# Encoder block on eight cores: the first sequence is read in halves of 256 positions, summed for its norm on TensorE, and projected in a new order

## The chip, the cores and the metric

The kernel runs on the eight cores of one Trainium2 chip. Each core works alone on two of sixteen sequences; no core talks to another. The metric is the device time in microseconds (us) of the slowest core, as a median of several runs. A profile is one execution, shown for the slowest core. The engines of a core are named as in the profile: PE (TensorE matmuls), PEld (its weight loads), ACT (ScalarE), DVE (VectorE), POOL (GpSimd) and SP (SyncE, which here only issues transfers). Each engine has its own queue and works through it in order; SPq, ACTq and POOLq are the queues as issuers of transfers.

## What is computed

One layer of a bidirectional encoder for x of 16 x 2048 positions x 1024 channels, in fp32 at the interface and bf16 in the matmuls:

```
h = RMSNorm(x)
[u | q | k | v | g_f | g_a] = h @ w_in        # 256 | 768 | 768 | 768 | 1024 | 1024
y_f = (real part of the 2-D DFT of u over positions and group channels) @ fourier_mix
y_a = three dilated windowed attentions (dilation 1, 4, 16; 4 heads of 64 each),
      partial rotary on q and k, combined by their softmax denominators
x = x + (sigmoid(g_f) * (y_f @ w_f) + sigmoid(g_a) * (y_a @ w_a)) @ w_mix_out
x = x + CrossAttn(RMSNorm(x), RMSNorm(mem))    # mem: 256 x 1024 per sequence
x = x + SqReLU_MLP(RMSNorm(x))                 # 1024 -> 4096 -> 1024
out = RMSNorm(x)
```

## The kernel before

All tensors lie with channels on the 128 partitions: `hT[:, c, t]` is channel chunk c of 8, position t of 2048. Every on-chip tile is a view of one buffer, the `arena`; a small planner (`Prog`) keeps the order of the program on each engine and adds a wait wherever two operations touch the same 256 bytes (or the same PSUM bank). Since a helper records every operation, all instructions carry line 148 (line 146 for groups of small transfers).

The two sequences run one after the other (`for b_ in range(nseq)`). For each: projection of u and of q, k of attention group 0 (256 columns each); v of group 0 (`v_unit`, 8 units); the DFT as folds on DVE (`folds`), a channel step (`z_unit`, `zx_unit`) and a position step (`dft_unit`, `dft_mid`); the rotary step, for which `gather` copies rows of q and k to a strip `rot` by 8 transfers on SP, `rotate` works on the strip on DVE, and 8 more transfers (kept in `back`) bring it home; attention group 0 with the projections of group 1 woven in (`interleave(attn(0), proj_gen(1), ...)`), then groups 1 and 2; the gates and branches (`gate_mm`, `branch`, n from 0 to 31, with the end of the attention, `combine`, still running on ACT and DVE when they begin); output projection, cross-attention, MLP. The second sequence's first norm is computed during the first sequence's MLP (`load_st`, `sq_st`, `load_xh`, `fin_next`), so its projection starts from a ready `hT`. The first sequence has nothing to hide behind, and the first stage of the program is its norm and projection.

In that first stage, x comes in four tiles `xin[tg]` of 512 positions, the first two in two halves of 256 columns. `norm1_sq` squares each of the 8 channel chunks on ACT and adds them in fp32 on DVE and POOL in two partial sums, splits the sum into a high and a low bf16 part, and `norm_rstd` adds over partitions with two matmuls against `ones`, followed by Ln and Exp on ACT; `norm_apply` writes `hT` with 8 DVE instructions. The projection is six units a tile (`u_unit` twice, `qk_unit` four times), each 8 matmuls into one PSUM bank and one copy on ACT. A list of hooks says after which unit the next norm's parts are put in. The memory's norm (`mem_sq`, `mem_fin`) is hooked to the last tile. Weights come by transfers of POOL's queue that also turn fp32 into bf16 (`aload(i)`: slice i of `wa`; 0 is u, 1 to 3 are q, k, v of group 0, 4 to 6 of group 1, 7 to 9 of group 2; `bload(i)` the larger ones). `aload(1)` and `aload(2)` stand behind POOL's additions of the first two halves, and the third and fourth tile of x wait for `aload(2)` to land.

The softmax here doesn't subtract the row's maximum and nothing guards it: scores larger than these inputs give would overflow.

## Time and profile before

| | |
|---|---|
| median of 3 runs (lowest to highest) | 2097.21 us (2095.4 to 2100.14) |
| the profiled execution's own time | 2097.6 us |
| its span, slowest core (core 7) | 2096.6 us |
| spans of the eight cores | 2087.0 to 2096.6 us |
| PE busy share of the span | 95% |
| mean granted clock of TensorE, by core | 0.981 to 0.985 |

The span runs from the first to the last instruction of the core; the time has 1.0 us more around it. A waiting row says which engine waited for which, in total, how many times, and the longest. A timeline row gives start, duration, engine, operation with its tile shapes and count, and in brackets how long the engine had been idle before it and who ended that. A row of windows gives busy time and count of each engine in a stretch, then the granted clock (1.00 is 2.4 GHz, 0.50 is 1.2 GHz), the busy share of the 16 transfer engines, and what they moved in GB/s.

### The profile page before, as it was taken

To read this page: it belongs to the slowest core of one execution; us is meant where nothing else is said; L and a number is where in the kernel's file an instruction comes from. 1 tells how busy PE (TensorE), PEld (TensorE's weight loads), DVE (VectorE), ACT (ScalarE), POOL (GpSimd) and SP (SyncE) were. 2 spreads that over 40 slices of the span, in tenths; PEclk is the share of its full clock that TensorE was granted. 3 is DMA by queue.
4 is the path that set the end of the run, shared out by engine and by line. 5 is a ranking of instruction groups with operands and counts; after the bars stand their busy time and mean duration, and the time that the engine had idled before them with its cause. 6 is when DMAs were issued, how large, how long until landed. Compare 5 with 4: busy or idle time off the path is not lost.

```text
span 2096.6 us, 30871 instructions; the slowest of 8 cores (2087.0 to 2096.6 us)
## 1 busy us (share of the span) xinstructions
PE 1983.2 (95%) x10282; PEld 973.3 (46%) x10282; DVE 982.1 (47%) x1586; ACT 770.7 (37%) x1309; POOL 418.5 (20%) x391
## 2 busy tenths in 40 slices
PE   4879979999999999999999997999999999999996
PEld 2445534455444444444445563445544444444443
DVE  4554663355554333334875467225645433333354
ACT  4434552246542143212434555224654211111243
POOL 2200013253240033100340001325314000000033
PEclk9999989999999999999999999999999999999998
DMA  8532226066100244223456322606610022222112
GB/s 208 126 76 61 48 40 194 1 112 117 34 21 40 41 121 109 52 61 72 142 140 151 61 41 41 201 1 107 121 36 1 1 41 41 41 41 41 21 71 91
DMA packets 40524, 155.43 MB, mean 74 GB/s; under 512 B 4785, under 2 KB 19250, under 8 KB 30130
## 3 DMA queue, kind: packets, MB, share of 16 engines
q0 software_dynamic: 11808, 75.50, 20.5%
q1 hardware_dynamic: 28128, 77.61, 11.9%
q8 instruction: 87, 1.43, 0.3%
q14 instruction: 67, 0.55, 0.1%
q10 hardware_dynamic: 434, 0.35, 0.1%
HBM read 205.87 MB, written 16.78 MB: 106 GB/s over the span
## 4 chain that ended last, share of the span: by engine, by line
PE 85%; DVE 5%; ACT 3%; issue 3%; DMA 2%; POOL 1%; SPq 1%; ACTq 0%; DVEq 0%; POOLq 0%
PE ps L148 85%; DVE arena L148 5%; ACT arena L148 3%; DMA arena<-arena 1%; POOL arena L148 1%; DMA arena<-x 1%; SPq L146 0%; DMA arena<-wa 0%; ACT L148 0%; ACTq L142 0%; DVEq L142 0%; SPq L148 0%; POOLq L142 0%; SPq L142 0%
## 5 line engine op out<-in xcount | busy, mean ns | idle before, releaser
L148 PE MATMUL ps<-arena 128*128 128x512 bf16 (+4 forms) x10282 | 1983.2, 355 | 105.3 <-ACT arena L148 57.6
L148 PEld LDWEIGHTS ps<-arena 128*128 128x128 bf16 (+1 forms) x10282 | 973.3, 100 | 1114.9 <-issue 188.7
L148 ACT ACTIVATE arena<-ps 128x512 bf16<-128x512 f32 (+4 forms) x812 | 488.9, 625 | 970.9 <-PE ps L148 803.9
L148 DVE TENSOR_TENSOR arena<-arena 128x512 bf16<-128x512 bf16 (+8 forms) x607 | 310.5, 531 | 604.2 <-ACT arena L148 586.2
L148 POOL TENSOR_TENSOR arena<-arena 128x512 f32<-128x512 f32 (+2 forms) x299 | 364.2, 1219 | 769.0 <-ACT arena L148 517.1
L148 DVE TENSOR_TENSOR arena<-ps,arena 128x512 f32<-128x512 f32 (+3 forms) x376 | 294.4, 791 | 244.2 <-PE ps L148 243.2
L148 ACT ACTIVATE arena<-arena 128x512 f32<-128x512 f32 (+3 forms) x451 | 261.3, 589 | 320.3 <-DVE arena L148 214.8
L148 DVE SCALAR_TENSOR_TENSOR arena<-arena 128x512 bf16<-128x512 f32 (+3 forms) x328 | 218.0, 707 | 51.0 <-ACT arena L148 50.5
L148 POOL DMA_DIRECT2D arena<-wb x62 | 33.6, 544 | 674.2 <-PE ps L148 674.1
L148 DVE SCALAR_TENSOR_TENSOR arena<-arena,ps 128x512 f32<-128x512 f32 x128 | 82.1, 684 | 151.7 <-PE ps L148 149.1
L148 DVE SCALAR_TENSOR_TENSOR arena<-ps,arena 128x512 f32<-128x512 f32 x64 | 43.5, 688 | 32.5 <-PE ps L148 32.5
L148 POOL DMA_DIRECT2D arena<-wa x20 | 10.9, 554 | 115.3 <-PE ps L148 113.9
L148 POOL MEMSET arena<- 128x2048 bf16 x6 | 10.9, 1812 | 109.3 <-PE ps L148 109.3
L148 ACT ACTIVATE arena<-ps,arena 128x512 f32<-128x512 f32 (+1 forms) x37 | 23.6, 637 | 24.8 <-PE ps L148 22.0
L148 DVE CAST arena<-ps 128x512 bf16<-128x512 f32 (+1 forms) x36 | 20.5, 582 | 11.8 <-PE ps L148 11.3
L148 DVE COPY arena<-ps 128x1024 f32<-128x1024 f32 (+3 forms) x20 | 20.2, 1010 | 6.6 <-PE ps L148 6.6
L148 DVE STREAM_SHUFFLE arena<-arena 128x2048 bf16<-128x2048 bf16 x6 | 13.7, 2288 | 0.0
L148 ACT ACT_TABLE_LOAD x9 | 11.5, 1283 | 2.9 <-PE ps L148 1.6
L148 DVE LOAD_MASK_SELECT arena<-arena x6 | 0.1, 14 | 7.2 <-DMA arena<-arena 7.2
L148 DVE CAST arena<-arena 128x1 bf16<-128x1 f32 (+1 forms) x9 | 1.4, 160 | 0.4
L148 DVE MEMSET arena<- 128x1 bf16 (+2 forms) x6 | 0.8, 130 | 1.2 <-PEq L211 1.1
L211 POOL MEMSET const-float32-0.0<- 128x1 f32 x1 | 0.1, 98 | 0.5 <-issue 0.5
(3 smaller groups left out, 0.3 us busy)
## 6 DMA issues: line engine op xcount, KB each, us to landing
arena<-wb POOLq DMA_DIRECT2D x62, 1024.0 KB, 10.1
arena<-x SPq DMA_DIRECT2D x40, 512.0 KB, 3.9
arena<-x SPq DMA_DIRECT2D x8, 2048.0 KB, 13.8
out<-arena SPq DMA_DIRECT2D x28, 512.0 KB, 2.7
arena<-wa POOLq DMA_DIRECT2D x20, 512.0 KB, 9.8
arena<-rope SPq DMA_DIRECT2D x6, 1024.0 KB, 9.7
arena<-arena SPq DMA_DIRECT2D x96, 64.0 KB, 2.3
arena<-x SPq DMA_DIRECT2D x16, 256.0 KB, 10.3
```

Of the source, the lines that this page charges most:

```text
L148: ins = getattr(eo, o['name'])(*o['args'], **o['kw'])
L211: nc = bass.Bass("TRN2", target_bir_lowering=False)
```

## The change

The input x is laid out as eight contiguous pieces of 256 positions a sequence instead of four of 512, and every transfer that reads x follows this. The rest concerns the first stage, the stage behind it, and one place in the gate stage:

- x of the first sequence is loaded as 8 halves (of 1 MB; SP issues half i once half i-2 has landed), the weights of u, q and k at once at the start, the other weights of the stage behind the last half, most constants behind half 5; `ones` is written by DVE.
- The squares go to bf16 tiles `sqb` by two ACT instructions of 1024 columns a half, and the sum over channels is taken by 8 matmuls against `ones` into one bank (`half_rstd`); the additions on DVE and POOL and the split in two parts are gone. `half_sum` does nothing.
- The projection works by halves: `tiles('uq', i)` keeps four banks open and walks over the channel chunks, `tiles('k', i)` two. Norms run one half ahead.
- `warm(n)` issues n matmuls of 128x512 whose result is not used: 10 at the start, 4 ahead of the first projection, 34 ahead of `branch(0)` in each sequence.
- Behind the projection the channel step is woven into the last four units of v, the DFT's position step follows directly, mostly in banks 2 to 5, and the memory's norm is finished there; the transfers of `aload(7)`, `bload(0)`, `bload(1)` and the next rotary table wait for `back`.

```diff
-    cb[:, 0:128] = 1.0
...
-    for name, shp, dt in [('x', [nseq, NTG, 128, 4096], F32), ('mem', [nseq, 128, 2048], F32),
+    for name, shp, dt in [('x', [nseq, 8, 128, 2048], F32), ('mem', [nseq, 128, 2048], F32),
...
         def load_consts():
             OP('dve', 'memset', eps, 1e-6, writes=[eps])
+            OP('dve', 'memset', ones, 1.0, writes=[ones])
+            OP('dve', 'memset', ones32, 1.0, writes=[ones32])
             act(rstd[:, 0:1], eps, AF.Square)
-            for q, dst, src in ((0, cb, dr['cb']), (1, gains, dr['gains'].rearrange("p (n c) -> p n c", n=5)),
-                                (2, fm32, dr['fmix']), (3, altrow[0:1, :], dr['altrow'])):
-                dma('act', dst, src, 'c%d' % q)
+            dma('act', gains, dr['gains'].rearrange("p (n c) -> p n c", n=5), 'c1')
             OP('dve', 'memset', Wz, 0.0, writes=[Wz])
+            warm(10)
+
+        def warm(n):
+            o = psf(P.bank())
+            for _ in range(n):
+                mm(o, ones, view(c0 + 2048, 512), True, True)
+
+        def load_consts2():
+            for q, dst, src in ((0, cb[:, 128:642], dr['cb'][:, 128:642]), (2, fm32, dr['fmix']), (3, altrow[0:1, :], dr['altrow'])):
+                dma('sp', dst, src, 'c%d' % q)
...
-        def norm_apply(gi, srcs, dsts, n=512):
+        def norm_apply(gi, srcs, dsts, n=512, r=None):
             for c in range(8):
-                stt(dsts[c], srcs[c], gains[:, gi, c:c + 1], rstd[:, 0:n], ALU.mult, ALU.mult)
+                stt(dsts[c], srcs[c], gains[:, gi, c:c + 1], rstd[:, 0:n] if r is None else r, ALU.mult, ALU.mult)
...
+        XOFF = [M0 + 16 * KB, M0 + 24 * KB, Y0, Y0 + 8 * KB] + [X0 + i * KB for i in (16, 24, 32, 40)]
+        xin = [view(o, 2048, F32, pat="p (c t) -> p c t", c=8) for o in XOFF]
+
+        def xpair(off, c):
+            return view(off, 4096, F32, pat="p (h c t) -> p h c t", h=2, c=8)[:, :, c, :]
+
+        def x_half(b_, i):
+            return dr['x'][b_, i].rearrange("p (c t) -> p c t", c=8)
+
+        xin_op = {}
+
+        def load_xin(i, parts=2):
+            for h in range(parts):
+                cs = slice(h * 8 // parts, (h + 1) * 8 // parts)
+                xin_op[i] = dma('sp', xin[i][:, cs, :], x_half(0, i)[:, cs, :], 'xin%d%d' % (i, h),
+                                [xin_op[i - 2]] if i > 1 else ())
+
+        sqb = [view(o, 2048) for o in (X0 + 48 * KB, X0 + 56 * KB, T0)]
+        ones32 = view(OFF['memn'], 128, F32)
+
+        def half_sq(i, parts=2, src=None):
+            n = 2048 // parts
+            src = (xin[i] if src is None else src).rearrange("p c t -> p (c t)")
+            for p in range(parts):
+                act(sqb[i % 3][:, p * n:(p + 1) * n], src[:, p * n:(p + 1) * n], AF.Square)
+
+        def half_sum(i):
+            q = sqb[i % 3]
+            return
+
+        def half_r(i):
+            return rstd[:, i % 2 * 256:i % 2 * 256 + 256]
+
+        def half_rstd(i, chunks=8):
+            o = psf(P.bank())[:, 0:256]
+            for c in range(chunks):
+                mm(o, ones, sqb[i % 3][:, c * 256:(c + 1) * 256], c == 0, c == chunks - 1)
+            act(half_r(i), o, AF.Ln, scale=1.0 / D, bias=eps)
+            act(half_r(i), half_r(i), AF.Exp, scale=-0.5)
+
+        def half_apply(i):
+            norm_apply(0, [xin[i][:, c, :] for c in range(8)], [hT[:, c, i * 256:(i + 1) * 256] for c in range(8)],
+                       256, half_r(i))
...
-                load_xin(0, 0, 0, 256)
+                load_xin(0, parts=4)
                 aload(0)
                 load_consts()
-                load_xin(0, 0, 256, 256)
-                load_xin(0, 1, 0, 256)
-                load_xin(0, 1, 256, 256)
-                norm1_sq(0, 0, ns=0, t0=0, n=256, eng=0)
-                norm1_fin(0, 0, 0, 0, 256)
                 aload(1)
-                norm1_sq(0, 0, ns=1, t0=256, n=256, eng=0)
-                wk = aload(2)
-                load_xin(0, 2, after=[wk])
-                load_xin(0, 3)
+                aload(2)
+                for i in range(1, 8):
+                    load_xin(i)
+                    if i == 5:
+                        load_consts2()
                 load_rope(0)
...
-            memst = view(X0 + 32 * KB, 2048, F32, pat="p (c m) -> p c m", c=8)
+            memst = view(Y0 + 8 * KB, 2048, F32, pat="p (c m) -> p c m", c=8)
...
-                tb = [ssacc, rstd][odd]
+                tb = view(T0 + 4096 + odd * 2048, 512, F32)
...
+                def tiles(which, i):
+                    tn = slice(i * 256, i * 256 + 256)
+                    us = [(aslot('uqk'.index(w)), j, psf(P.bank())[:, 0:256], w) for w in which for j in range(2)]
+                    for dc in range(8):
+                        for w, j, o, _ in us:
+                            mm(o, w[:, dc, j * 128:(j + 1) * 128], hT[:, dc, tn], dc == 0, dc == 7)
+                    for _, j, o, w in us:
+                        if w == 'u':
+                            act(uT[:, j, tn], o, AF.Copy)
+                        else:
+                            cp('act', qkv_views(0)['qk'.index(w)][:, j, tn], o)
+
+                half_sq(0, parts=4)
+                half_rstd(0, 8)
+                half_apply(0)
+                half_sq(1)
+                warm(4)
+                tiles('uq', 0)
+                half_sq(2)
+                half_rstd(1, 8)
+                half_apply(1)
+                half_sq(3)
+                half_sum(3)
+                aload(3, [xin_op[7]])
+                tiles('uq', 1)
+                half_rstd(2, 8)
+                half_apply(2)
+                tiles('k', 0)
+                tiles('k', 1)
+                for i in range(2, 8):
+                    if i < 7:
+                        half_rstd(i + 1)
+                        half_apply(i + 1)
+                    if i == 2:
+                        half_sq(4)
+                        half_sum(4)
+                    tiles('uq', i)
+                    if i < 5:
+                        half_sq(i + 3)
+                        half_sum(i + 3)
+                    if 3 < i < 7:
+                        aload(i, [xin_op[7]])
+                    if i == 6:
+                        v_ones(0)
+                        load_dft()
+                    if i == 7:
+                        make_wz()
+                        half_sq(8, src=memst)
+                        half_sum(8)
+                    tiles('k', i)
...
             for i in range(8):
                 v_unit(0, 2 * i, ALLB)
+                if i == 5 and b_ == 0:
+                    half_rstd(8)
+                if i > 3:
+                    z_unit(i - 4, 0)
             zx_unit()
-            for i in range(4):
-                z_unit(i, 0)
-                z_unit(i, 1)
+            LB = (2, 3, 4, 5)
+            z_unit(0, 1)
+            z_unit(1, 1)
+            dft_unit(0, 0, ALLB)
+            z_unit(2, 1)
+            z_unit(3, 1)
+            dft_unit(0, 1, LB)
+            dft_mid(LB)
+            dft_unit(1, 0, LB)
+            dft_unit(1, 1, LB)
+            if b_ == 0:
+                norm_apply(2, [memst[:, c, :] for c in range(8)], [memn[:, c, :] for c in range(8)], 256, half_r(8))
             v_ones(1)
-            bload(0)
-            bload(1)
-            load_rope(1)
+            if b_ == 0:
+                aload(7, back.values())
+            bload(0, back.values())
+            bload(1, back.values())
+            load_rope(1, back.values())
...
-            for j in range(2):
-                for odd in range(2):
-                    dft_unit(j, odd, ALLB)
-            dft_mid(ALLB)
...
+                if n == 0:
+                    warm(34)
                 branch(n)
                 if n == 6:
                     for tg in range(NTG):
-                        dma('sp', xT[:, tg], dr['x'][b_, tg].rearrange("p (c t) -> p c t", c=8), 'xr%d' % tg)
+                        for h in range(2):
+                            dma('sp', xT[:, tg, :, h * 256:(h + 1) * 256], x_half(b_, 2 * tg + h), 'xr%d%d' % (tg, h))
...
-                for h in range(4):
-                    dma('sp', xst[:, 2 * h:2 * h + 2, :], dr['x'][b_ + 1, tg].rearrange("p (c t) -> p c t", c=8)[:, 2 * h:2 * h + 2, :], 'st%d' % h)
+                for h in range(2):
+                    dma('sp', xst[h], x_half(b_ + 1, 2 * tg + h), 'st%d' % h)
...
-                norm_sq(fc, xst[:, fc, :], ns=1)
+                norm_sq(fc, xpair(M0 + 16384, fc), ns=1)
...
+                dma('sp', xh[i % 3], x_half(b_ + 1, i), 'xh%d' % (i % 3))
...
-    xl = x.reshape(B, NTG, 512, 8, 128).transpose(0, 1, 4, 3, 2).reshape(B, NTG, 128, 4096)
+    xl = x.reshape(B, 8, 256, 8, 128).transpose(0, 1, 4, 3, 2).reshape(B, 8, 128, 2048)
```

## Rows read from the trace of the kernel before

**Rows 1.** Windows: first projection, v of group 0, then up to the first attention.

```profile
0.00:98.20 98.20, 60.96 (x308) 32.67 (x309) 47.62 (x90) 44.47 (x111) 27.88 (x38) 0.91 0.72 175
98.20:112.20 14.00, 13.99 (x129) 12.29 (x126) 11.00 (x23) 6.28 (x12) 0.00 (x0) 1.00 0.23 40
112.20:135.24 23.04, 11.26 (x78) 5.69 (x79) 14.30 (x21) 7.67 (x15) 2.86 (x3) 0.91 0.68 126
```

**Rows 2.** Waits of PE up to 98 us: in total, times, longest.

```profile
PE ps L148 <- ACT arena L148: 26.1, 6, 17.7
PE ps L148 <- DVE arena L148: 9.7, 13, 2.2
```

**Rows 3.** The chain that ended last: first transfer of x.

```profile
2.56 12.11 DMA arena<-x
```

**Rows 4.** Timeline of the first stage: one instruction or run of each kind.

```profile
20.66 1.06 PE L148 MATMUL ps<-arena 128*128 128x256 bf16 x3 [2.11 <-DVE arena L148]
...
29.65 3.25 DVE L148 SCALAR_TENSOR_TENSOR arena<-arena 128x256 bf16<-128x256 f32 x8 [1.77 <-ACT arena L148]
...
32.37 4.53 PE L148 MATMUL ps<-arena 128*128 128x256 bf16 x40 [0.56 <-DMA arena<-wa]
...
37.07 1.19 ACT L148 ACTIVATE arena<-ps 128x256 bf16<-128x256 f32 x4
...
43.29 0.47 ACT L148 ACTIVATE arena<-ps,arena 128x256 f32<-128x256 f32 x1
...
69.76 4.31 ACT L148 ACTIVATE arena<-arena 128x512 f32<-128x512 f32 x8
```

**Rows 5.** Transfer queues up to 100 us: packets, MB, share of 16 engines.

```profile
q1 hardware_dynamic: 5936, 12.58, 43.7%
q0 software_dynamic: 1152, 4.19, 25.8%
```

**Rows 6.** Windows inside the first stage.

```profile
46.00:52.00 6.00, 5.88 (x25) 3.34 (x25) 4.75 (x12) 4.12 (x9) 0.74 (x1) 0.50 1.04 238
52.00:54.00 2.00, 2.00 (x19) 1.70 (x17) 2.00 (x2) 0.16 (x1) 1.80 (x2) 0.91 1.10 199
...
66.00:68.00 2.00, 1.71 (x4) 0.31 (x3) 2.00 (x4) 0.00 (x0) 0.00 (x0) 0.51 0.63 125
```

**Rows 7.** Timeline from the end of the projection to the first attention.

```profile
96.69 15.50 PE L148 MATMUL ps<-arena 128*128 128x512 bf16 x135
...
100.67 3.26 DVE L148 SCALAR_TENSOR_TENSOR arena<-arena 128x256 bf16<-128x256 f32 x8 [2.88 <-ACT arena L148]
...
115.30 2.06 PE L148 MATMUL ps<-arena 128*128 128x128 bf16 x27 [0.39 <-DVE arena L148]
...
117.86 3.69 DVE L148 TENSOR_TENSOR arena<-arena 128x2048 bf16<-128x2048 bf16 x3 [0.17 <-DVE arena L148]
...
118.86 7.74 PE L148 MATMUL ps<-arena 128*128 128x512 bf16 x41 [0.60 <-ACT arena L148]
...
135.24 15.09 PE L148 MATMUL ps<-arena 64*128 64x192 bf16 x69 [8.65 <-DMA arena<-arena]
```

**Rows 8.** Small transfers of the rotary step, median to landing: 118 to 140 us.

```profile
arena<-arena SPq DMA_DIRECT2D x8, 64.0 KB, 10.2
```

**Rows 9.** The same transfers over the whole span (the page).

```profile
arena<-arena SPq DMA_DIRECT2D x96, 64.0 KB, 2.3
```

**Rows 10.** Timeline of PE at the first branches, first sequence, then second.

```profile
304.14 8.06 PE L148 MATMUL ps<-arena 128*128 128x512 bf16 x27 [8.11 <-ACT arena L148]
...
1285.15 12.78 PE L148 MATMUL ps<-arena 128*128 128x512 bf16 x52 [2.27 <-DVE arena L148]
1301.88 10.35 PE L148 MATMUL ps<-arena 128*128 128x512 bf16 x40 [3.96 <-ACT arena L148]
```

**Rows 11.** Timeline of ACT behind v in the second sequence.

```profile
1129.41 4.67 ACT L148 ACTIVATE arena<-ps 128x512 bf16<-128x512 f32 x10 [1.15 <-PE ps L148]
```

**Rows 12.** Window of the gate stage behind the second reading of x.

```profile
340.00:345.00 5.00, 5.00 (x25) 2.25 (x23) 1.31 (x3) 1.68 (x3) 1.26 (x1) 1.00 0.00 0
```

More of the change, by code:

```diff
@@ L340, in norm_sq, with like @@
             acc_, hi, lo = acc_[:, 0:n], hi[:, 0:n], lo[:, 0:n]
+            def like(a):
+                return a if len(src.shape) == 2 else a.rearrange("p (h t) -> p h t", h=2)
             if isinstance(eng, int):
@@ L346, in norm_sq @@
                 b = sq4[k % 4][:, 0:n]
-                act(part if k < 2 else b, src, AF.Square)
+                act(like(part if k < 2 else b), src, AF.Square)
                 if k > 1:
@@ L358, in add @@
                     tt(eng, acc_, acc_, sq[i % 2][:, 0:n], ALU.add)
-            act(sq[k % 2][:, 0:n] if k else acc_, src, AF.Square)
+            act(like(sq[k % 2][:, 0:n] if k else acc_), src, AF.Square)
             if lag and k:
@@ L411, in build_program @@
         rope = view(R0 + 32768, 4096, pat="p (k t) -> p k t", k=2)
-        xin = [view(o, 4096, F32, pat="p (c t) -> p c t", c=8) for o in (M0 + 16384, Y0, X0 + 16 * KB, X0 + 32 * KB)]
-        def load_xin(b_, tg, t0=0, n=512, after=()):
-            src = dr['x'][b_, tg].rearrange("p (c t) -> p c t", c=8)
-            i = tg
-            return [dma('sp', xin[i][:, 2 * h:2 * h + 2, t0:t0 + n], src[:, 2 * h:2 * h + 2, t0:t0 + n],
-                        'xin%d%d%d' % (i, h, t0), after) for h in range(4)]
@@ L431, in build_program, with load_rope @@
         rsw = view(X0 + 60 * KB, 2048)
[L433 to L434 removed]
+        def load_rope(g, after=()):
+            dma('sp', rope, dr['rope'][g].rearrange("p (k t) -> p k t", k=2), 'rope', after)
         pend = []
@@ L1079, in load_xh @@
             def load_xh(i):
-                tg, t0 = i // 2, i % 2 * 256
-                for h in range(2):
-                    dma('sp', xh[i % 3][:, 4 * h:4 * h + 4, :],
-                        dr['x'][b_ + 1, tg].rearrange("p (c t) -> p c t", c=8)[:, 4 * h:4 * h + 4, t0:t0 + 256], 'xh%d%d' % (i % 3, h))
+                dma('sp', xh[i % 3], x_half(b_ + 1, i), 'xh%d' % (i % 3))
             def fin_next(tg, b_=b_):
```

40 lines of the change are left out of this document (2 added, 38 removed).

## The prediction

> **What bounds the kernel now.** I began with the windows by stage [rows 1], because a busy share over the whole span hides where PE stands idle. The reader is to see that the first 98.2 us hold 61.0 us of PE work, and that the 23 us ahead of the first attention hold 11.3 us; the 14 us of v between them are full. A window of the gate stage [rows 12] shows PE busy all the time, as most of the rest; there only matmuls count, and no part of the change removes one of those. What can be gained lies in the two stretches in front.
>
> The waits of PE in the first stretch [rows 2] say on whom: 26.1 us for ACT (17.7 of them at the start, when ACT itself waits for x) and 9.7 us for DVE. The chain [rows 3] begins with a transfer of x from 2.56 to 14.67 us; the first projection matmul runs at 20.66 [rows 4]. So 6.0 us pass from the landing of the first 256 positions to work for PE, and the same path of squares, additions, splitting, Ln, Exp and scaling stands ahead of every later half. Transfers are busy 72% of the stretch [rows 1]; the last x lands at about 67 us, where their share falls to 0.63 [rows 6]. By the queues [rows 5] plain transfers take 43.7 us of all engines for 12.58 MB, 3.47 us a MB, and the converting ones 25.8 us for 4.19 MB, 6.16 us a MB.
>
> In the second stretch PE waits 8.65 us at the end for the rotary strip's way home [rows 7], which took 10.2 us to land [rows 8] where the same transfers take 2.3 us over the span [rows 9]: two large weight loads and a table were issued beside them.
>
> **The change, part by part. The start.** One half of x (1.05 MB) costs 3.64 us of the queue, one converting load (0.52 MB) 3.23 us. Three converting loads now run beside the first halves instead of one. Half 0 can't land before 2.56 + 3.64 = 6.2 us, and before the change 14.7 us were needed; I take 11.5. From there: a square of 512 columns 0.54 (4.31 / 8), the last two sum matmuls 0.4, Ln 0.47, Exp no dearer, one scaling 0.41 (3.25 / 8) [rows 4], and five handoffs of 0.1: the projection starts at 14.4 and its 32 matmuls take 32 x 0.113 = 3.6 us (4.53 / 40), to 18.0. The additions on POOL and DVE and the split are gone from the path; the 8 sum matmuls cost PE 8 x 0.108 = 0.87 us a half (13.99 / 129 [rows 1]) where it had two.
>
> **The second half waits for the third.** In ACT's order the squares of half 2 stand ahead of Ln and Exp of half 1; while x of half 2 is missing, the norm of half 1 waits behind it. Until half 2 has landed the engines move 3.15 MB of x (10.9 us) and 1.57 MB of weights (9.7 us): 2.56 + 20.6 = 23.2 us; without the weights it would be 13.5. I take 23.2. Two squares of 1024 columns (at most 2 x 0.54 each) 2.1, Ln and Exp 0.9, one scaling 0.4: `tiles('uq', 1)` starts at 26.7.
>
> **From there PE is the bound.** A half costs PE 48 x 0.113 + 0.87 = 6.3 us; ACT 2.1 + six copies of 0.30 (1.19 / 4) + 0.9 = 4.8; DVE 3.3; the x queue 3.64. SP issues a half only when the one two before has landed, which keeps two in flight; x is through after 8.39 x 3.47 + 9.7 = 38.8 us, at about 42, ahead of need. Behind 26.7 come: `uq` of half 1 3.6, sum of half 2 0.9, `k` of halves 0 and 1 3.6, sum of half 3 0.9, six halves of 5.42 32.5, four sums 3.5, and the wait for `make_wz` ahead of the last `k`, which I put at 1.3 (its matmuls stand behind a DVE cast, as before): 46.3, to 73.0. Seven us of idle PE ahead of 26.7 may cost clock: between 46 and 52 us the granted clock was 0.50 and 25 matmuls of 256 took 6 us, when 19 took 2 right behind [rows 6]. At 0.113 they would have taken 2.8, so one such fall costs 3.2; I book half, 1.5. The projection ends at 74.5 instead of 98.2: **23.7 gained**; at best 66.7 (half 2 early, no fall, no wait for `make_wz`).
>
> **v to attention.** Before, 37.0 us (98.2 to 135.24). PE's work: v 14.0, channel step 32 x 0.076 = 2.4 (2.06 / 27 [rows 7]), memory sum 0.9, `zx` 0.3, position step 33 matmuls of 512 at 0.217 = 7.2, `dft_mid` 0.6: 25.4, and 2 for handoffs between short steps: 27.4. The other path is DVE's: folds and rotary step took 103.9 to 121.55, 17.6 us [rows 7], and start as the projection ends, since the memory's 8 scalings (3.26 us) no longer stand ahead. From the end of `rotate` to attention went 13.7 us, 10.2 of it landing and 3.5 issue; with 2.3 for landing it is 5.8. Sum 23.4, under PE's 27.4: the way home is hidden with 4 us to spare, and if it lands in 10.2 again it shows by 4. **9.6 gained**, between 7 and 11.6. What waits for `back` now: on POOL three weight loads with nothing due behind them until the next group's weights, on SP the rotary table, needed only near the end of attention group 0. So I cost these waits at nothing; the cover is that stage's PE work.
>
> **Small terms.** The memory's 8 scalings now lie on DVE ahead of the first attention masks: between 0 and 3.3, I take 1 lost. `warm(34)` is 34 x 0.217 = 7.4 us of PE. In the first sequence PE stood 8.11 us idle there, in the second 3.96 [rows 10]: nothing in the first, 3.4 in the second, less the slow matmuls after the idle time; I take 3 lost, between 0 and 7. In the second sequence half of the channel step's copies (4.67 us on ACT [rows 11]) goes beneath v, while PE's part of it, 1.2, lengthens v: 1 gained, between 0 and 3. The second reading of x now lands in rows of 1 KB; it is issued at n = 6 with 25 rounds of 20 matmuls (4.3 us each) ahead of its first use, and was through by 340 us with PE full [rows 12]: nothing, and even at half speed nothing. The contiguous loads in the MLP lie under full PE: nothing.
>
> **Sum.** 23.7 + 9.6 - 1 - 3 + 1 = 30.3 us off the profiled execution's 2097.6: 2067.3. The median shown is 0.4 below that execution: 2067.
>
> **Clock, row and rule.** The row shows 1.2 GHz for 6 us of which PE was busy 5.88, behind a stretch of short bursts, and then a rise to 0.91 of 2.4 GHz [rows 6]. The Trainium skill (TensorE: Matmul & The Clock Gate, section "HAM oscillation — how this bites in real kernels") says that a loop which waits between short bursts falls back at each wait, and that every burst then starts slow. By that rule the woven order could start half after half slow; the sum goes by the row, one fall booked by half, and the rule's case is the fifth way below.
>
> **The other ways it could go.** (1) As summed, 2060 to 2075. (2) Half 2 lands early and no clock falls: 66.7 and 25.4 behind it, 43.1 gained in the two stretches; with the small losses hidden and 2 from the second sequence 2052. For it speaks that squares and x overlap far better; against it the three converting loads at once. (3) x lands no earlier than before, at 67: then squares, sum, Ln, Exp and the last half's projection follow, 67 + 2.1 + 0.9 + 0.9 + 0.4 + 5.4 + 1.3 = 78.0, 3.5 worse, 2071; with two falls of the clock 2077. Against it: the first stretch moved x in rows of 1 or 2 KB, paused for `aload(2)`, and shared with five more weight loads that now wait. (4) The second stretch keeps its 37 us, because something else ends there last (the DFT matrix late, small transfers slow again): 2077. (5) Slower: PE stays at 1.2 GHz through the first stretch. Matmuls then double from 26.7 on, 45.0 more: 118.0, attention at 145.4, 10 later than before, with the small terms 2111. It decides when more than 70% of that work (31.8 of 45.0 us, where attention plus 3 reaches 135.24) runs slow; the rows show 0.91 as the stretch's mean clock with far more idle time, so it is unlikely. That nothing changes would need two of these in balance.
>
> **How the numbers follow.** Chances: (1) 0.55, (2) 0.15, (3) 0.14, (4) 0.11, (5) 0.03, no change 0.02. The time is that of (1), 2067. The worst of (3) with 30 us for the second stretch and `warm(34)` uncovered is 2087; the range from 2052 to 2080 leaves out the far ends of (2) and (3), and (5). Within 0.2% (4.2 us) counts as no change, about what a measurement of this kernel can tell: faster 0.95, same 0.02, slower 0.03.
>
> **What would show it.** In the profile after, the last projection matmul near 74 and the first of attention near 102; x landed by 45; PE without waits for ACT between 27 and 73; the strip's small transfers landing in 2 to 3 us; in the second sequence branches beginning some 3 us later against the end of attention. I am wrong if x lands after 60, if the granted clock is 0.50 for more than 10 us of the stretch, or if attention begins more than 32 us after the last projection.

## The result, and the profile after

| | before | after |
|---|---|---|
| time, median of the runs | 2097.66 us | 2058.13 us |
| ratio of the times, 95% interval | | 0.9809 [0.9773, 0.9844] |
| profiled execution | 2097.6 us | 2056.9 us |
| span of the slowest core | 2096.6 us (core 7) | 2055.9 us (core 1) |
| mean span of the 8 cores | 2091.7 us | 2053.3 us |

The forecast was 2067 us, from 2052 to 2080. The change is faster by 40 us, 9 more than forecast. The same kernel on another chip, beside the last experiments, gave a ratio of 0.9800 [0.9786, 0.9814]. The pages of before and after show different cores, and cores differ by some microseconds at the start, so the stages below are means over cores: a stage begins where a named instruction begins. On the chips of the experiments one die ran at a lower clock in many runs, so an experiment's means are over four cores of the other die (0 to 3, for the last four 4 to 7), in its profiled execution or, where it is said, in all executions in which that die kept its clock.

| start in us (mean) | first scaling | second half's scaling | first copy of v | to first Exp of attention | group 0: on to POOL's memset for group 2 | from there to the end | span |
|---|---|---|---|---|---|---|---|
| before | 19.9 | 29.7 | 100.6 | 34.3 | 60.0 | 1896.9 | 2091.7 |
| after | 20.4 | 29.6 | 79.1 | 23.5 | 56.8 | 1893.9 | 2053.3 |
| gained | -0.4 | 0.0 | 21.4 | 10.7 | 3.2 | 3.0 | 38.4 |
| forecast | 6 | 3 | 23.7 | 9.6 | 0 | -3 | 30.3 |

The columns after the third are durations and add up with it to the span. In the last row, the memory's scalings (-1) and `warm(34)` and the second sequence (-3 and +1) stand together.

The windows of core 1 answer to [rows 1]: the projection up to v, v, and up to the first Exp.

```profile
0.00:78.20 78.20, 60.20 (x470) 47.65 (x471) 28.92 (x78) 39.87 (x84) 5.88 (x12) 0.87 0.81 205
78.20:92.20 14.00, 14.00 (x137) 12.62 (x135) 12.97 (x25) 6.85 (x15) 0.00 (x0) 1.00 0.29 79
92.20:103.63 11.43, 11.43 (x83) 5.97 (x81) 8.14 (x10) 6.24 (x13) 1.80 (x1) 1.00 0.28 47
```

PE's busy time in the projection is as before (60.2 against 61.0 us); 19 us of idle time are gone. Behind v PE is now full, where it stood half idle. The idle time that is left lies ahead of 31 us. The timeline of PE on this core shows it, and below it PE's timeline behind 66 us and its waits up to 66 us, which answer to [rows 2].

```profile
2.19 4.08 PE L148 MATMUL ps<-arena 128*128 128x512 bf16 x10 [2.19 <-DVE arena L148]
...
19.35 2.29 PE L148 MATMUL ps<-arena 128*128 128x256 bf16 x6 [4.88 <-ACT arena L148]
22.06 4.90 PE L148 MATMUL ps<-arena 128*128 128x256 bf16 x40 [0.42 <-DVE arena L148]
30.62 35.55 PE L148 MATMUL ps<-arena 128*128 128x256 bf16 x298 [3.67 <-DVE arena L148]
```

```profile
75.86 28.40 PE L148 MATMUL ps<-arena 128*128 128x256 bf16 x237 [0.18 <-ACT arena L148]
```

```profile
PE ps L148 <- ACT arena L148: 11.5, 4, 4.9
PE ps L148 <- DVE arena L148: 6.3, 3, 3.7
```

Two things differ from the forecast there. The last quarter of the first half of x is squared at 18.58 us (mean of the cores 17.6), as soon as it has landed; the forecast had it landed at 11.5. And the 3.67 us ahead of the second half are not a wait for x. The timeline of ACT shows what stands there:

```profile
18.58 0.63 ACT L148 ACTIVATE arena<-arena 128x512 bf16<-128x512 f32 x1 [4.83 <-DMA arena<-x]
...
22.09 1.06 ACT L148 ACTIVATE arena<-arena 128x1024 bf16<-128x1024 f32 x1 [1.01 <-DMA arena<-x]
23.34 1.06 ACT L148 ACTIVATE arena<-arena 128x1024 bf16<-128x1024 f32 x1 [0.20 <-DMA arena<-x]
25.85 1.21 ACT L148 ACTIVATE arena<-ps 128x256 f32<-128x256 f32 x4 [1.45 <-PE ps L148]
26.93 2.02 ACT L148 ACTIVATE arena<-arena 128x1024 bf16<-128x1024 f32 x2
28.82 0.50 ACT L148 ACTIVATE arena<-ps,arena 128x256 f32<-128x256 f32 x1
```

The two squares of the third half (26.93) follow the copies without a wait, so its x had landed; the Ln of the second half (28.82), which PE waits for, stands behind them. The strip's transfers land in 2.3 us (10.2 in [rows 8]):

```profile
arena<-arena SPq DMA_DIRECT2D x8, 64.0 KB, 2.3
```

### The profile page after: what moved, and what is told of

Read it like the earlier page. It is cut to its first block, busy times and chain, and to the rows that moved or that the text cites. A ratio compares the mean times of both kernels' runs of the same rounds, so it can differ in the third digit from the quotient of the medians.

```text
span 2055.9 us, 31118 instructions; the slowest of 8 cores (2052.1 to 2055.9 us)
## 1 busy us (share of the span) xinstructions
PE 1988.6 (97%) x10518; PEld 993.4 (48%) x10518; DVE 963.2 (47%) x1573; ACT 765.1 (37%) x1282; POOL 397.4 (19%) x366
## 4 chain that ended last, share of the span: by engine, by line
PE 90%; DVE 3%; ACT 3%; issue 2%; DMA 1%; POOL 0%; SPq 0%; ACTq 0%; DVEq 0%; POOLq 0%
PE ps L148 90%; DVE arena L148 3%; ACT arena L148 2%; DMA arena<-x 1%; DMA arena<-arena 0%; POOL arena L148 0%; SPq L146 0%; ACT L148 0%; ACTq L142 0%; DVEq L142 0%; SPq L148 0%; POOLq L142 0%; SPq L142 0%
## 5 line engine op out<-in xcount | busy, mean ns | idle before, releaser
L148 PE MATMUL ps<-arena 128*128 128x512 bf16 (+5 forms) x10518 | 1988.6, 352 | 60.0 <-ACT arena L148 31.4
L148 PEld LDWEIGHTS ps<-arena 128*128 128x128 bf16 (+1 forms) x10518 | 993.4, 100 | 1055.0 <-issue 125.7
L148 ACT ACTIVATE arena<-ps 128x512 bf16<-128x512 f32 (+5 forms) x824 | 489.7, 618 | 948.7 <-PE ps L148 788.4
L148 DVE TENSOR_TENSOR arena<-arena 128x512 bf16<-128x512 bf16 (+7 forms) x576 | 294.4, 532 | 554.7 <-ACT arena L148 542.7
L148 POOL TENSOR_TENSOR arena<-arena 128x512 f32<-128x512 f32 (+2 forms) x274 | 343.1, 1254 | 699.8 <-ACT arena L148 450.3
L148 ACT ACTIVATE arena<-arena 128x512 f32<-128x512 f32 (+5 forms) x410 | 254.5, 625 | 310.5 <-DVE arena L148 196.8
L148 DVE SCALAR_TENSOR_TENSOR arena<-arena 128x256 bf16<-128x256 f32 (+3 forms) x344 | 215.9, 672 | 80.8 <-ACT arena L148 80.4
L148 DVE CAST arena<-ps 128x512 bf16<-128x512 f32 (+1 forms) x36 | 20.5, 582 | 15.8 <-PE ps L148 15.3
L148 ACT ACT_TABLE_LOAD x9 | 11.5, 1283 | 2.9 <-PE ps L148 1.6
```

The costliest lines, as they stand in the source:

```text
L148: ins = getattr(eo, o['name'])(*o['args'], **o['kw'])
```

## The experiments

Stages of all of them, in the columns of the table above (mean over four cores), and the ratio of whole runs where one was obtained:

| run | first scaling | second scaling | first copy of v | to first Exp | group 0 | span | ratio to before, 95% |
|---|---|---|---|---|---|---|---|
| without warm(34) | 19.7 | 29.0 | 77.7 | 23.5 | 56.6 | 2054.8 | - |
| without warm(10), warm(4) | 19.9 | 30.6 | 79.1 | 23.5 | 56.7 | 2056.4 | 0.9833 [0.9813, 0.9852] |
| no wait for `back` | 19.8 | 29.1 | 78.3 | 23.5 | 56.5 | 2052.4 | 0.9808 [0.9786, 0.9831] |
| third weight load later | 19.4 | 30.6 | 80.0 | 23.5 | 56.9 | 2054.6 | 0.9828 [0.9805, 0.9850] |
| memory first | 21.0 | 30.0 | 80.4 | 26.0 | 56.8 | 2059.3 | - |
| memory first, no wait | 19.7 | 29.1 | 78.8 | 33.9 | 58.3 | 2064.2 | - |
| Ln ahead of squares | 20.4 | 27.8 | 75.0 | 23.5 | 56.8 | 2049.7 | - |
| second half waits for first | 19.7 | 30.2 | 79.7 | 23.5 | 56.5 | 2053.4 | - |
| after, again | 19.1 | 28.3 | 77.5 | 23.5 | 56.2 | 2051.6 | 0.9800 [0.9786, 0.9814] |
| first half in 8 KB rows | 16.0 | 28.3 | 76.9 | 23.8 | 56.9 | 2052.1 | 0.9811 [0.9797, 0.9825] |
| 8 KB rows and Ln ahead | 17.0 | 27.6 | 74.5 | 23.8 | 56.9 | 2050.2 | 0.9789 [0.9776, 0.9803] |
| weights not held back | 20.3 | 40.6 | 90.0 | 23.5 | 56.9 | 2064.0 | 0.9855 [0.9838, 0.9872] |

The kernel after stands at 79.1 (all cores), 79.6 (0 to 3) and 77.5 (again, 4 to 7) in the column of v, so differences under some 2 us say nothing there; the column behind it repeats to 0.01 us.

**Without `warm(34)`.**

```diff
-                if n == 0:
-                    warm(34)
```

> The kernel after without the 34 extra matmuls of warm(34) ahead of branch(0), in both sequences; nothing else changes. Theory of the forecast: in the second sequence the 7.4 us of these matmuls stand 3 us longer than what they cover, so without them the time falls by about 3 us, to 2055 (span of the slowest core near 2053). Rival: the matmuls lie wholly beside ACT's combine chain in both sequences; then PE's wait ahead of the first branch returns at 7 to 9 us where it now is 1.0, the first branch begins when it does now, and the time is the same to 2.5 us longer, the extra being gate matmuls that run at a granted clock under 1.0 behind the idle time (2058 to 2060.5).

PE at the first branch of the second sequence, without the matmuls (core 1), and a window there:

```profile
1238.83 11.83 PE L148 MATMUL ps<-arena 128*128 128x128 bf16 x60 [1.30 <-DVE arena L148]
1258.45 41.80 PE L148 MATMUL ps<-arena 128*128 128x512 bf16 x182 [7.79 <-ACT arena L148]
...
1258.00:1264.00 6.00, 5.54 (x15) 2.00 (x16) 5.05 (x8) 2.76 (x6) 3.57 (x3) 0.56 0.00 1
```

With them, in the kernel after (core 1):

```profile
1243.18 18.74 PE L148 MATMUL ps<-arena 128*128 128x128 bf16 x92 [1.43 <-DVE arena L148]
1262.92 37.29 PE L148 MATMUL ps<-arena 128*128 128x512 bf16 x171 [1.00 <-ACT arena L148]
...
1263.00:1269.00 6.00, 6.00 (x28) 2.58 (x28) 5.43 (x10) 2.11 (x5) 4.53 (x4) 1.00 0.02 4
```

From the start of the gates to the branch it takes 19.62 us without the matmuls and 19.74 with them: ACT's chain ends it either way, in both sequences. What the matmuls buy shows behind it: 28 matmuls of the branches in 6 us against 15. The granted clock there is 1.00 against 0.56, nearly the lower level of 1.2 GHz. Between POOL's marks the stage of gates and first branches is 1.1 us longer without them in the first sequence (148.1 against 147.0, cores 0 to 3) and 0.6 in the second; single cores differ there by up to 3 us, so the stage alone doesn't settle it. The mean span of these cores over all executions does: 2055.1 us without the matmuls (three executions), and 2052.3 and 2053.7 in the two runs on the same chip that change nothing at this place (no wait for `back`, five; third weight load later, four). The forecast had 3 us lost; between 1.4 and 2.8 are gained. The Trainium skill (TensorE: Matmul & The Clock Gate, section "HAM oscillation — how this bites in real kernels") says that a burst behind a wait starts slow; the trace agrees.

**Without the warming at the start.**

```diff
-            warm(10)
...
-                warm(4)
```

> The kernel after without warm(10) and warm(4) in the first 22 us; nothing else changes. Theory: they buy nothing, since the granted clock in the profile after was 0.50 from 10 to 22 us anyway, between the end of warm(10) at 6.3 us and the first projection: the first projection matmul, the second half's start and the end of the projection stay within 1 us, time within 1 us of 2058. Rival: they set the clock of the first projection; without them its 40 matmuls take up to 4.5 us longer (0.122 us each at the clock they got, 0.23 at 0.50 of 2.4 GHz), and the whole stretch starts as much later if the second half doesn't wait for x anyway.

The first copy of v lies at 79.1, as with them: they bought nothing here. The span is some 3 us longer all the same (2056.5 over four executions, beside the 2052.3 and 2053.7 above), and the trace puts that in another place, the gates of the second sequence. PE on core 0, a window, and ACT on core 0, here and then in the kernel after:

```profile
1241.74 0.61 PE L148 MATMUL ps<-arena 128*128 128x128 bf16 x8 [1.49 <-DVE arena L148]
1244.63 65.64 PE L148 MATMUL ps<-arena 128*128 128x512 bf16 x284 [2.28 <-DVE arena L148]
...
1245.00:1255.00 10.00, 9.95 (x34) 3.97 (x34) 6.29 (x10) 8.98 (x15) 0.00 (x0) 0.72 0.01 2
```

```profile
1260.62 3.05 ACT L148 ACTIVATE arena<-ps 128x512 f32<-128x512 f32 x6
1274.88 0.60 ACT L148 ACTIVATE arena<-ps 128x512 f32<-128x512 f32 x1 [11.21 <-PE ps L148]
```

```profile
1260.25 3.04 ACT L148 ACTIVATE arena<-ps 128x512 f32<-128x512 f32 x6
1270.16 1.08 ACT L148 ACTIVATE arena<-ps 128x512 f32<-128x512 f32 x2 [6.87 <-PE ps L148]
```

This wait of 2.28 us stands in the second sequence of the kernel before too (2.27, [rows 10]), and not in the kernel after. It comes from the code: `P.bank()` gives out the eight PSUM banks in turn, and attention's output always lies in banks 4 and 5 (`ob = 4`). Counting the calls, the first gate tile behind the last attention group gets bank 4 in the second sequence of the kernel before, 7 in the kernel after, 6 without `warm(34)`, and 5 here, since two `warm` calls fewer take a bank. With 4 or 5 it waits for DVE's last reading of that bank, on all eight cores, and with 7 on none, nor with 6 on cores 0 to 3. Then the clock falls (0.72, 34 matmuls in 10 us where the kernel after makes 47), and PE is late. In the kernel after PE's wait ahead of the branch ends with the first of ACT's six activations at 1260.25. Here these begin 0.4 us later (1260.62), but ACT's next work, which waits for PE, begins 4.7 us later: PE now ends last, by some 4 us, less than the 7.4 us of the 34 matmuls. Between two of POOL's weight loads around it the stage takes 92.1 us here, 88.0 in the kernel after, 88.7 without `warm(34)`, and 87.4 in the kernel before, which has the wait but not the matmuls (cores 0 to 3). So the matmuls cost some 4 us where the bank makes PE late, and nothing where it doesn't.

**No wait for the way home, and the memory put back first.** Three runs separate the parts of the second stretch.

```diff
-                aload(7, back.values())
-            bload(0, back.values())
-            bload(1, back.values())
-            load_rope(1, back.values())
+                aload(7)
+            bload(0)
+            bload(1)
+            load_rope(1)
```

> The kernel after in which the weight loads 7, 0 and 1 of that stage and the rotary table no longer wait for the rotary strip's way home. Theory of the forecast: the strip's transfers land in about 10 us again instead of 2 to 3, which shows by 4 us: first attention near 107 to 108 instead of 103, time about 2062. The rival is that the order of the stage (DFT work behind the rotation) hides even the slow landing: then the first attention begins within 1 us of now and the time stays at 2058, whatever the landing takes. A second question is where the unforeseen 3 to 4.6 us inside the first attention group come from: if they come from these waits, they go here (the later markers lose 3 us more than the first attention does).

```diff
+            if b_ == 0:
+                half_rstd(8)
+                norm_apply(2, [memst[:, c, :] for c in range(8)], [memn[:, c, :] for c in range(8)], 256, half_r(8))
             gather(0, 0)
             gather(0, 1)
             folds()
...
-                if i == 5 and b_ == 0:
-                    half_rstd(8)
...
-            if b_ == 0:
-                norm_apply(2, [memst[:, c, :] for c in range(8)], [memn[:, c, :] for c in range(8)], 256, half_r(8))
```

> The kernel after with the memory's sum, Ln, Exp and 8 scalings put back ahead of the folds, where the kernel before had them; the waits for the strip's way home stay. DVE's path to the first attention then begins some 4 to 5 us later. Theory: the second stretch got short because DVE's path starts at once, and with the strip landing in 2 to 3 us only about 2 us of the delay show: fold to first Exp unchanged and first Exp 4 to 6 us after where it is now measured from the end of the projection, time about 2060 to 2063. Rival, by the forecast's sum: PE has 4 us to spare over DVE's path there, so the scalings are hidden and the time stays at 2058 (the order of z and the position step would then be what shortened the stretch).

> As the run before, and the three weight loads and the rotary table don't wait for the strip's way home either. Theory: what the waits buy depends on who is issued first; with the memory ahead DVE ends its rotary step after the weight loads are issued, the strip lands in about 10 us as in the kernel before (in 2.3 to 5.7 where only the waits were taken out), PE waits 5 to 9 us ahead of the first attention, and the first attention group loses 2 to 4 us more behind that wait (time 2068 to 2072). Rival: the strip is no slower than without the waits alone, and the time is that of the run before.

The strip's transfers on core 0: without the waits alone, with the memory first, and with both.

```profile
arena<-arena SPq DMA_DIRECT2D x8, 64.0 KB, 5.7
```

```profile
arena<-arena SPq DMA_DIRECT2D x10, 64.0 KB, 2.4
```

```profile
arena<-arena SPq DMA_DIRECT2D x8, 64.0 KB, 10.4
```

PE ahead of the first attention with both edits, and the window behind it (core 0). The last two lines are the 6 us behind the first attention in the kernel before (core 7) and after (core 1).

```profile
103.39 1.89 PE L148 MATMUL ps<-arena 128*128 128x512 bf16 x8 [1.24 <-DVE arena L148]
114.60 15.52 PE L148 MATMUL ps<-arena 64*128 64x192 bf16 x78 [9.32 <-DMA arena<-arena]
...
115.20:121.20 6.00, 6.00 (x22) 2.11 (x22) 0.69 (x2) 1.96 (x3) 0.00 (x0) 0.68 0.97 285
```

```profile
136.00:142.00 6.00, 6.00 (x16) 2.01 (x16) 0.69 (x2) 1.51 (x2) 0.00 (x0) 0.57 0.26 107
```

```profile
103.60:109.60 6.00, 6.00 (x34) 2.62 (x34) 5.74 (x14) 3.31 (x5) 1.59 (x3) 1.00 0.64 180
```

With both the stage is 33.9 us long, that of the kernel before is 34.3. Here DVE ends its rotary step at 100.25 us, and POOL issues its weights from 99.63 on. Either cure alone suffices nearly: the waits bring it to 26.0, the memory out of the way to 23.5, and both to 23.5. In the kernel after the waits are worth nothing: without them DVE is done 3 us before POOL issues (95.8 against 98.8 on core 0), the strip lands in 5.7 us, and PE's work covers that. With the memory first and the waits kept, the 2.5 us that remain are four waits of PE for DVE ahead of attention (0.26, 0.60, 0.39 and 1.24 us): DVE's folds and rotary step come late, not the strip. The 9 us wait also costs behind it: the clock there is 0.68, with 22 matmuls in 6 us instead of 34, and attention group 0 takes 58.3 us instead of 56.8. The kernel before shows the same behind its wait of 8.65 us (0.57, 16 matmuls).

**Ln ahead of squares.** In the program's order the second half's Ln, Exp and scaling change places with the third half's squares.

```diff
-                half_sq(2)
                 half_rstd(1, 8)
                 half_apply(1)
+                half_sq(2)
                 half_sq(3)
```

> The kernel after with Ln, Exp and scaling of the second half of x ahead of the squares of the third half in the program's order (half_rstd(1) and half_apply(1) ahead of half_sq(2)). Theory: the second half's projection waits on ACT's two squares of 1.06 us, not on the landing of the third half; PE's idle 3.7 us ahead of it falls to 1.5, and the projection ends 2 us earlier, time about 2056. Rival: the third half has not landed then, or the clock falls all the same and gives it back: the projection's end moves by less than 0.5 us.

ACT and PE on core 1:

```profile
25.09 1.21 ACT L148 ACTIVATE arena<-ps 128x256 f32<-128x256 f32 x4 [2.59 <-PE ps L148]
26.29 0.47 ACT L148 ACTIVATE arena<-ps,arena 128x256 f32<-128x256 f32 x1
...
28.07 38.15 PE L148 MATMUL ps<-arena 128*128 128x256 bf16 x348 [1.88 <-DVE arena L148]
```

Windows of 6 us behind the wait, first here and then in the kernel after (core 1 of both):

```profile
28.00:34.00 6.00, 5.93 (x55) 5.32 (x56) 2.69 (x7) 5.12 (x10) 0.00 (x0) 1.00 0.96 308
```

```profile
30.00:36.00 6.00, 5.38 (x26) 3.85 (x27) 3.25 (x8) 1.83 (x2) 0.00 (x0) 0.50 0.92 276
```

PE's wait is 1.88 us on all four cores, where it was 3.66, and v begins over 4 us earlier (75.0 against 79.6 in the kernel after, and 79.7 in the run below whose second half waits, on the same chip). So the order was the cause. 1.8 us are the wait itself; the rest is clock: behind 1.88 us without work the granted clock is 1.00, behind 3.67 us it is 0.50 for the next 6 us (0.50 to 0.75 on cores 0 to 3), and PE makes 26 matmuls instead of 55. That is this place alone and no rule: on core 0 of the kernel after the clock stayed at 1.00 through a wait of 4.36 us ahead of 14.24. The forecast had booked half of one such fall. The mean span of the four cores is 3.7 us shorter than in that run, and 5.0 over all executions (2049.0 in five against 2054.0 in three).

**What holds the first half of x.** Six runs: the third weight load behind the first half, the second half behind the first, the kernel after again, the first half in one transfer, that with the order above and the second half in one transfer too, and the weights 3 to 6 not held back.

```diff
-                aload(2)
+                aload(2, [xin_op[0]])
```

> The kernel after with the third converting weight load (aload(2), needed by the first k tile only) issued when the first half of x has landed. Theory that the converting loads share the transfer engines by turns with x: the first half's last part lands at least 3 us earlier than its 18.5 us, the first projection starts as much earlier, and the projection ends 2 to 3 us earlier (v from 75 to 76 instead of 78.2 on the slowest core), time about 2055. Rival: the first half is paced by its own queue or by the first two converting loads, and nothing moves by more than 1 us; or k of the first half waits for its late weights and the gain is lost there (a PE wait ahead of the first k matmuls of more than 2 us).

```diff
-                                [xin_op[i - 2]] if i > 1 else ())
+                                [xin_op[i - 2]] if i > 1 else [xin_op[0]] if i else ())
```

> The kernel after with the second half of x issued when the first has landed, instead of right behind it. Theory: the two halves and three converting loads share the engines, which is why the first half lands at 16.7 to 19.5 us and not at the 11.5 forecast; alone with the converting loads it lands 3 to 5 us earlier (first scaling at 16 instead of 20.4). The second half lands no earlier than now, so the second half's projection starts within 1 us of now or up to 2 us later, and the time stays within 2 us of 2058. Rival: the first half is paced by the converting loads alone and lands when it does now; then the second half is 3 to 4 us later, and so is the time (2061 to 2062).

Neither moves the first scaling by more than 1.4 us against the kernel after on cores 0 to 3 (20.8). With the third weight load later PE waits 4.3 to 7.1 us ahead of the second half, because x of the third half comes later: nothing is gained. The queues of the kernel after between 8 and 16 us (core 1) gave the next idea (packets, MB, share of the engines):

```profile
q0 software_dynamic: 297, 1.09, 78.3%
q1 hardware_dynamic: 295, 0.59, 25.4%
```

The packet counts are equal, 297 and 295, and the shares are not; on none of the eight cores do the two counts differ by more than 10. A packet of a converting load took 0.34 us of an engine (an estimate: 78.3% of 16 x 8 us, by 297) and one of x 0.11: whoever sends small packets gets little. The Trainium skill (DMA: Bandwidth & Descriptors, section "Queues, rings and completion order") says that each engine goes round its queues packet by packet; the counts agree. Whether a packet that the profile counts, here one row of x, is what that page calls a packet, no run here shows.

```diff
-                load_xin(0, parts=4)
+                load_xin(0, parts=1)
```

> The kernel after, unchanged, beside the three runs that follow on the same chip. Both theories: first scaling near 20.4 us, second half's scaling near 29.6, first copy of v near 79, first Exp 23.5 behind it, as in the profile after (means over cores); the spans of undisturbed cores 2050 to 2056.

> The kernel after with the first half of x loaded in one transfer of rows of 8 KB instead of four of rows of 2 KB; its squares in four parts as before. Theory: while converting loads are queued each transfer engine takes one packet of either queue in turn; the rows show 75 packets of x (2 KB, 0.09 us each) against 76 converting ones (0.33 us each) in 2 us, so x gets a fifth of the engines, and with 8 KB packets (0.37 us) it would get half. The first half then lands by 12 to 14 us instead of 16.7 to 19.5, the first scaling starts at 15.5 to 17.5 instead of 20.4 although its squares can't start ahead of the whole, and the weights land some 2 us later. The end of the projection hangs on the second half and moves by at most 2 us. Rival: the first half is paced by something else (its bytes, or the rate of its queue) and lands within 1 us of now; without the early parts the first scaling is then 1 to 2 us later.

Queues between 8 and 12 us, then ACT and PE (core 4), then the queues between 4 and 6 us, here and in the kernel after again (core 4 of both):

```profile
q0 software_dynamic: 96, 0.39, 65.7%
q1 hardware_dynamic: 93, 0.33, 28.6%
```

```profile
8.05 2.19 ACT L148 ACTIVATE arena<-arena 128x512 bf16<-128x512 f32 x4 [5.28 <-DMA arena<-x]
15.27 0.47 ACT L148 ACTIVATE arena<-ps,arena 128x256 f32<-128x256 f32 x1 [5.03 <-DMA arena<-gains]
...
19.60 5.92 PE L148 MATMUL ps<-arena 128*128 128x256 bf16 x38 [1.78 <-DMA arena<-wa]
29.55 36.65 PE L148 MATMUL ps<-arena 128*128 128x256 bf16 x319 [4.03 <-DVE arena L148]
```

```profile
q1 hardware_dynamic: 91, 0.68, 107.5%
```

```profile
q0 software_dynamic: 32, 0.13, 76.5%
q1 hardware_dynamic: 66, 0.11, 31.0%
```

The first half has landed at 8 us (6.7 to 8.9 on the four cores) instead of 17, so its rows were what held it. But it also beats the 12 to 14 us that the theory of turns gave, and the turns are not what this run tests: by 6 us 1.00 to 1.18 MB of x had moved and at most 4 converting packets, so the half was through before the turns began. In the kernel after on the same chip 0.54 to 0.55 MB of x and 30 to 38 converting packets had moved by then, and the rest of the half went by turns. Why the converting loads begin later beside large rows was not tried. The early landing doesn't help, since the next two things then end last: the gains (20 KB, ready at 15.3 us) and the second weight load (19.6 us). The second scaling stays at 28.3.

> The kernel after with both first halves of x in single transfers of rows of 8 KB, and with Ln, Exp and scaling of the second half ahead of the squares of the third half (the order of the earlier run on this, whose second scaling began at 27.5 and whose projection ended 4 us earlier than that of the kernel after). Theory of turns: the second half lands at about 20 instead of 22 to 23, its scaling begins at 24 to 25, v some 7 us earlier than in the kernel after (first copy of v near 72), spans of undisturbed cores near 2046 to 2048. Rival: the order alone gives what is to be had and the larger packets nothing: first copy of v near 75, spans near 2050.

The edit is the order of above and `parts=1` for the first two halves. Here the turns are seen with larger rows: between 8 and 16 us 190 packets of x moved 1.02 MB beside 196 converting ones with 0.74 MB (core 4), where the kernel after again moved 0.45 to 0.72 MB of x on its eight cores. The run gave 2060.3 us and a ratio of 0.9789 [0.9776, 0.9803], beside 0.9800 [0.9786, 0.9814] for the kernel after on the same chip: v begins 2.9 us earlier, no more than the order gave by itself, and the larger packets add nothing, as the rival had it. By the ratios it is 2.3 us quicker than the kernel after (0.0011 x 2105), the lowest ratio that was obtained; the intervals overlap, so that it is quicker is not shown by them.

```diff
-                aload(3, [xin_op[7]])
+                aload(3)
...
-                        aload(i, [xin_op[7]])
+                        aload(i)
```

> The kernel after in which the next four converting loads (3 to 6) don't wait until the last half of x has landed; they are issued right behind the first three. Theory of turns: seven converting loads hold the engines until about 32 to 36 us, x gets a fifth to a third of them for so long, the second half lands at 27 to 29 instead of 22.7 and the third at 35 or later; the second half's scaling begins at 36 or later instead of 29.6 and the projection ends 6 us later (first copy of v near 85), time 2063 to 2066. Rival: x has 25 us to spare over PE in the kernel after (landed by 46, needed by 70), the deferral is worth nothing and the time stays at 2058.

Queues between 20 and 32 us, ACT, and PE (core 4):

```profile
q0 software_dynamic: 374, 1.37, 65.6%
q1 hardware_dynamic: 373, 1.36, 37.8%
```

```profile
32.22 1.06 ACT L148 ACTIVATE arena<-arena 128x1024 bf16<-128x1024 f32 x1 [2.58 <-DMA arena<-x]
37.42 1.06 ACT L148 ACTIVATE arena<-arena 128x1024 bf16<-128x1024 f32 x1 [4.14 <-DMA arena<-x]
...
40.15 40.01 PE L148 MATMUL ps<-arena 128*128 128x256 bf16 x342 [10.45 <-DVE arena L148]
```

Equal counts again. The ratio is 0.9855 [0.9838, 0.9872], 11.6 us more than that of the kernel after (0.0055 x 2105), and v begins 12.5 us later. Holding four weight loads back is worth more than half of what the first stretch gained; the 6 us expected were too little, because the third half's squares (37.42), which wait for its x, stand ahead of the second half's Ln here too. The rival with 25 us to spare is out: time to spare at the last half doesn't help the second and third.

## Why the prediction was right, and where its sum was off

- **The start: wrong, in the step "I take 11.5".** The first half's landing was chosen between 6.2 and 14.7 without a sum, from costs per MB; it landed at 17.6, later than both. x came in rows of 2 KB, and while converting loads had work the engines moved as many packets of one queue as of the other. So the projection starts 6 us later than forecast.
- **"The second half waits for the third": right that its norm stands behind the third half's squares, wrong that x is missing.** `tiles('uq', 1)` starts at 30.6 instead of 26.7 on core 1, because of the late start and of ACT's order; changing the order gave 4 us.
- **"From there PE is the bound": right, with two terms that offset each other.** From 30.62 to v at 78.2 are 47.6 us, forecast 46.3 and 1.5. But the clock's fall cost about 3 us, not 1.5 (26 matmuls in 6 us where 55 fit), and the wait for `make_wz`, booked at 1.3, is not there: behind 31 us PE waits once, for 0.18. x had landed by 43 to 48 us (POOL's weights, issued on it). The first stretch gave 21.4 of 23.7.
- **A sign of being wrong that came true.** The granted clock was 0.50 for more than 10 us of the stretch: added up over windows of 1 us, for 17 to 21 us on five cores (on core 1 between 10 and 22 us and between 30 and 36), and for 3 to 7 on the other three. On core 1 most of that lies ahead of 22 us, where PE has little to do, so it cost little there; the part behind 30 us is the fall that cost about 3 us.
- **v to attention: right, 10.7 of 9.6.** That PE is the bound there, and that the way home is hidden, is shown by the run without the waits, whose strip lands later and whose stage is as long. From v to the first attention matmul it takes 24.9 us on core 1 (78.20 to 103.14), forecast 27.4: PE is busy throughout, and the 2 us for handoffs are not there. Attention so begins at 102.2 (mean), forecast 101.9, although the projection ends later than forecast; that the two errors cancel is luck. The forecast gave the gain to PE's order, DVE's earlier start and the waits together. PE's order by itself gives 0.4 (33.9 against 34.3), with the waits 8.3, with DVE's earlier start all of it.
- **`warm(34)`: the term with the largest error.** Forecast -3; without the matmuls the kernel after is 1.4 to 2.8 us longer. The 3.96 us idle of the second sequence [rows 10] was short because PE was late by a wait for a PSUM bank and by the clock. The change moved the bank, and with it the price. The run without the early warming, where the wait is back, shows a loss of some 4. From before to after the stage of gates and first branches is 1.9 us shorter in the first sequence (148.6 to 146.7, all cores) and 0.6 longer in the second (87.6 to 88.1).
- **Attention group 0: 3.2 us, not in the sum.** 1.5 are what a long wait ahead of it costs in clock, shown by the run with both edits. In the kernel before PE also waits for DVE some 50 us into the group, up to 2.9 us on a core, after up to 1.3; what that is from was not tried.
- **The small terms** were right for the second sequence's v (1.1 of 1) and the loads of x later on (0); the memory's scalings cost nothing seen.

Sum of the differences: -2.3 + 1.1 + 3.2, and 6.0 for all that lies behind group 0, make 8.0 us, which is 38.4 less 30.3 up to rounding. The other 2 us of the profiled executions are the slowest core: before it lay 4.9 us above the mean, after 2.6. Of the rivals the early one (2052) had its second stretch, not its first; x no earlier, 37 us kept, and a slow PE did not come. So the two stretches that the forecast was about came out at 32.1 of 33.3 us; the 9 us more than forecast lie behind them.

## What to carry to other kernels

Price a transfer that runs beside others by its packets and theirs, not by its bytes alone, and hold back the loads that nobody waits for yet. Read from an in-order engine's list what stands ahead of the instruction that frees the bound engine: here a place in the list was worth 4 us. Where banks are given out in turn, a tile more or less, anywhere ahead, can move another tile onto a bank that is still being read; look at the banks when a wait appears far from an edit.

## What the runs showed of the hardware

While both queues had work, the transfer engines moved nearly equal numbers of packets from each (297 and 295, 96 and 93, 374 and 373, 196 and 190), with rows of x between 2 and 8 KB. A 20 KB table in rows of 160 bytes was ready only at 13.5 to 16.2 us (four cores), later than 1 MB in rows of 8 KB that had landed at 6.7 to 8.9. Behind 7.8 us without work PE ran its next 15 matmuls of 512 columns at 0.56 of its clock; with 34 spare matmuls in the gap it made 28 in that time.
